# A two-layer hybrid decoder trunk: LoRA over 96 stacked rows, the norm's weights spread by all rows, and a new order of the shifts around the key norm

## The reference

```python
def rwkv7_time_mix(p, mu, w0, w2, a0, a2, k_k, k_a, r_k, lnx_w, lnx_b):
    p = p + (token_shift(p) - p) * mu
    r, k, v, wl, al = jnp.split(p, [G, 2 * G, 3 * G, 3 * G + L], axis=-1)
    decay = jnp.exp(-RWKV_DECAY_SCALE * jax.nn.sigmoid(w0 + jnp.tanh(wl) @ w2))
    a = jax.nn.sigmoid(a0 + al @ a2)
    kk = (k * k_k).reshape(B, T, H, N).astype(jnp.float32)
    kk = kk / jnp.maximum(jnp.sqrt(jnp.sum(kk * kk, axis=-1, keepdims=True)), 1e-12)
    k = k * (1.0 + (a - 1.0) * k_a)
    ...
```

## Time and profile before

| | us |
|---|---|
| median of 3 runs | 575.93 |
| lowest and highest | 575.54, 576.25 |
| the profiled execution's own time | 576.12 |
| its span in the profile | 574.3 |
| TensorE busy (share of the span) | 565.8 (99%) |
| VectorE, ScalarE, POOL busy | 379.9, 277.8, 249.5 |

### The profile page before, as it was taken

The page is one execution under the profiler, slowest core; times in us unless marked ns, Lnnn a source line. Parts: engine busy times, 40 slices in busy tenths (PEclk is TensorE's granted clock), DMA queues, the critical chain, the costliest instruction groups (busy, mean ns, idle before and its releaser), DMA issues. The chain is left out here.

```text
span 574.3 us, 12717 instructions
## 1 busy us (share of the span) xinstructions
PE 565.8 (99%) x5230; PEld 461.7 (80%) x5230; DVE 379.9 (66%) x644; ACT 277.8 (48%) x555; POOL 249.5 (43%) x197
## 2 busy tenths in 40 slices
PE   8999999999999999999999999999999999999995
PEld 6978888888877777888898788888888777788884
DVE  4989986482488557774444897947436865778173
ACT  6486241343574474534657643324357335735253
POOL 4937552044941322536335455402386313145340
PEclk9999999999999999999999999999999999999999
DMA  9546634056432122354544433332743321224513
GB/s 281 160 125 204 218 99 111 9 130 149 107 81 75 39 75 72 100 180 130 162 123 134 111 78 107 89 69 59 163 128 80 79 71 39 73 75 147 181 43 143
DMA packets 103374, 64.58 MB, mean 112 GB/s; under 512 B 29152, under 2 KB 94228, under 8 KB 103317
## 3 DMA queue, kind: packets, MB, share of 16 engines
q1 hardware_dynamic: 103316, 63.77, 39.9%
HBM read 55.61 MB, written 8.14 MB: 111 GB/s over the span
## 5 line engine op out<-in xcount | busy, mean ns | idle before, releaser
L706 POOL TENSOR_TENSOR w_lo<-w_raw,w_hi 128x512 fp32r<-128x512 f32 x156 | 216.7, 1408 | 282.2 <-ACT w_hi L1307 280.7
L770 PE MATMUL bank<-act_hi,w_hi 128*128 128x512 f32 x432 | 173.2, 401 | 0.0
L773 PE MATMUL bank<-act_lo,w_hi 128*128 128x512 f32 x432 | 168.5, 390 | 0.0
L772 PE MATMUL bank<-act_hi,w_lo 128*128 128x512 f32 x416 | 162.3, 390 | 0.0
L1307 ACT ACTIVATE w_hi<-w_raw 128x512 fp32r<-128x512 f32 x140 | 80.2, 621 | 78.3 <-PE bank L869 28.2
L770 PEld LDWEIGHTS bank<-act_hi,w_hi 128*128 128x128 f32 x432 | 81.1, 188 | 24.8 <-issue 8.4
L773 PEld LDWEIGHTS bank<-act_lo,w_hi 128*128 128x128 f32 x432 | 81.1, 188 | 17.4
L772 PEld LDWEIGHTS bank<-act_hi,w_lo 128*128 128x128 f32 x416 | 78.2, 188 | 14.9
L1233 PE MATMUL bank<-w_hi,act_hi 128*128 128x512 f32 x128 | 50.0, 391 | 0.0
L1235 PE MATMUL bank<-w_hi,act_lo 128*128 128x512 f32 x128 | 49.8, 389 | 0.0
L1234 PE MATMUL bank<-w_lo,act_hi 128*128 128x512 f32 x128 | 49.8, 389 | 0.0
(11 more groups left out here) (223 smaller groups left out, 946.2 us busy)
## 6 DMA issues: line engine op xcount, KB each, us to landing
w_raw<-in_w_in_dram SPq DMA_DIRECT2D x62, 512.0 KB, 4.0
w_raw<-in_w_out_dram SPq DMA_DIRECT2D x16, 512.0 KB, 3.8
pages<-in_x_dram SPq DMA_DIRECT2D x4, 512.0 KB, 6.2
x_or_y<-in_x_dram SPq DMA_DIRECT2D x4, 512.0 KB, 3.9
x_scratch<-x_or_y SPq DMA_DIRECT2D x4, 512.0 KB, 3.1
x_or_y<-x_scratch SPq DMA_DIRECT2D x4, 512.0 KB, 3.7
out_dram<-pages SPq DMA_DIRECT2D x8, 256.0 KB, 2.2
bias_scratch<-pages SPq DMA_DIRECT2D x1, 1280.0 KB, 7.5
```

Source lines behind the costliest of these rows:

```text
L706: ins = pool.tensor_tensor(low, raw, w_hi[:, i % HI, k, 0:n].bitcast(F32), ALU.subtract)
L770: mm(b[:, :], hi, act_hi[:, k, :], start=n == 0, stop=False)
L772: mm(b[:, :], lo, act_hi[:, k, :], start=False, stop=False)
L773: ins = mm(b[:, :], hi, act_lo[:, k, :], start=False, stop=n == KT - 1)
```

## The change

It changes five things. LoRA: the weights of both products are rounded and stacked in 96 rows as high, low and high, the inputs as high, high and low, so that one matmul in the one-pass format does what full precision did; the parts are made by a copy on ScalarE and a subtraction on VectorE (weights, first layer only) and by four copies on ScalarE and two subtractions on VectorE (inputs). The start: the norm's row lies on top of a page of zeros, so the ones span 128 rows; that load and the bias table's are issued by ScalarE, after the page has been cleared by VectorE and POOL; six idle products instead of four. The bias: the last two parts of its rows are made before the first norm, the second behind r0. The key norm: `kk_unit` is cut in two, with r1's shift between the parts. The order: LoRA comes behind v0, the decay scan behind v1, and the split parts and the product of the bonus move behind the next copies.

```diff
@@ layer_steps
-          ("kk_norm",), ("kk_unit", 0), ("lora_tanh",), ("shift", "r1"), ("kk_unit", 1), ("lora",), ("shift", "v0"), ("decay_scan",), ("shift", "v1"),
+          ("kk_norm",), ("kk_unit", 0), ("lora_tanh",), ("lora_low",), ("shift", "r1"), ("kk_scale", 0), ("shift", "v0"), ("lora",), ("kk_unit", 1), ("kk_scale", 1), ("shift", "v1"), ("decay_scan",),
           ("decay_exp",), ("factors", 0), ("gate", "rwkv", 0), ("factors", 1), ("gate", "rwkv", 1), ("factors", 2)]
 
-    s += [("copy", "rq0"), ("copy", "rq1"), ("bonus",), ("rotate", "rq0"),
-          ("copy", "rk0"), ("rotate", "rq1"), ("scores", 0), ("scores", 1), ...
+    s += [("copy", "rq0"), ("rkv_parts",), ("copy", "rq1"), ("rotate", "rq0"),
+          ("copy", "rk0"), ("rotate", "rq1"), ("bonus",), ("scores", 0), ("scores", 1), ...
@@ buffers
-        lora_w = sb("lora_w", [4 * LORA, DEPTH, P])
+        lora_w = sb("lora_w", [3 * LORA, 2, DEPTH, G], F32R)
-        norm_row = page(10)[0:1]
+        norm_rows = page(10)
+        lora_raw = page(2)[0:3 * LORA].rearrange("p (z l c) -> p z l c", z=2, l=DEPTH)
@@ SP
-            load(norm_row, norm_w[0:1, :], "norm_loaded")
-            load(bias_table, rel_bias.partition_broadcast(P), "bias_in")
-            for p in range(2):
-                for r, w in ((2 * p, rwkv_w2), (2 * p + 1, rwkv_a2)):
-                    load(lora_w[r * LORA:(r + 1) * LORA], w[:, :, p * P:(p + 1) * P].rearrange("l k c -> k l c"), "const_b")
+            for r in range(3):
+                for z, w in enumerate((rwkv_w2, rwkv_a2)):
+                    load(lora_raw[r * LORA:(r + 1) * LORA, z], w.rearrange("l k c -> k l c"), "lora_loaded")
@@ POOL
+            pool.memset(norm_rows[:, T:2 * T], 0.0).then_inc(s("norm_clear"), 1)
@@ TensorE
-            idle(4)
+            idle(6)
-                end(mm(b[:, :], one[0:1, :].to_broadcast([1, P]), norm_row[:, a * T:(a + 1) * T], start=True, stop=True), f"nw{a}", -1)
+                end(mm(b[:, :], one.to_broadcast([P, P]), norm_rows[:, a * T:(a + 1) * T], start=True, stop=True), f"nw{a}", -1)
...
-                    pe.wait_ge(*at("lora_in", layer))
-                    for p in range(2):
-                        for z, r0 in (("zw", 2 * p * LORA), ("za", (2 * p + 1) * LORA)):
-                            b = begin(f"{z}{p}", layer)
-                            end(mm(b[:, :], lora_w[r0:r0 + LORA, layer, :], WA[r0:r0 + LORA, :], start=True, stop=True, tile_position=(r0, 0)), f"{z}{p}", layer)
+                    for p in range(2):
+                        for z, name in enumerate(("zw", "za")):
+                            pe.wait_ge(*at("lora_in", layer, 2 - z))
+                            b = begin(f"{name}{p}", layer)
+                            end(mm(b[:, :], lora_w[:, z, layer, p * P:(p + 1) * P], stat_hi[0:3 * LORA, z, :], start=True, stop=True), f"{name}{p}", layer)
@@ ScalarE
+            act.wait_ge(s("norm_clear"), 2)
+            act.dma_start(norm_rows[0:1], norm_w[0:1, :]).then_inc(s("norm_loaded"), 16)
+            act.dma_start(bias_table, rel_bias.partition_broadcast(P)).then_inc(s("bias_in"), 16)
...
+                    if layer == 0:
+                        act.wait_ge(s("lora_loaded"), 16 * 6)
+                        go(lora_w.rearrange("p z l c -> p (z l c)"), lora_raw.rearrange("p z l c -> p (z l c)"), ACT.Copy).then_inc(s("lora_weight"), 1)
...
-                    go(WA[2 * LORA:4 * LORA], WA[0:2 * LORA], ACT.Copy).then_inc(s("lora_copied"), 1)
-                    act.wait_ge(*at("lora_copied", layer))
-                    for r0 in (0, 2 * LORA):
-                        go(WA[r0:r0 + LORA], WA[r0:r0 + LORA], ACT.Tanh).then_inc(s("lora_in"), 1)
+                    go(WA[0:LORA], WA[0:LORA], ACT.Tanh).then_inc(s("lora_bent"), 1)
+                    for z in (1, 0):
+                        if z == 0:
+                            act.wait_ge(*at("lora_bent", layer))
+                        for r in range(2):
+                            go(stat_hi[r * LORA:(r + 1) * LORA, z, :], WA[z * LORA:(z + 1) * LORA], ACT.Copy).then_inc(s("lora_high"), 1)
@@ VectorE
+            dve.memset(norm_rows[:, 0:T], 0.0).then_inc(s("norm_clear"), 1)
             dve.memset(bias_rows[:, :, T:DIST], MASKED)
...
+            dve.wait_ge(s("bias_in"), 16)
+            bias_runs(2)
+            bias_runs(3)
             for two in (0, 2):
...
                         if layer == 0:
-                            bias_runs(3)
+                            dve.wait_ge(s("lora_weight"), 1)
+                            low = slice(LORA, 2 * LORA)
+                            tt(lora_w[low], lora_raw[low], lora_w[low].bitcast(F32), ALU.subtract).then_inc(s("lora_weight"), 1)
...
-                    if layer == 0 and job in ("k0", "k1"):
-                        bias_runs(int(job[1]))
+                    if layer == 0 and job in ("k0", "r0"):
+                        bias_runs(0 if job == "k0" else 1)
...
                     link(dve.reciprocal(KN[:, p, :], KN[:, p, :]))
+
+                def kk_scale(p):
                     stt(KN[:, p, :], K[:, p, :], par[:, layer, KKP + p:KKP + p + 1], KN[:, p, :], ALU.mult, ALU.mult).then_inc(s("kk_unit"), 1)
+
+                def lora_low():
+                    for z in (1, 0):
+                        dve.wait_ge(*at("lora_high", layer, 4 - 2 * z))
+                        r = slice(z * LORA, (z + 1) * LORA)
+                        tt(stat_hi[2 * LORA:3 * LORA, z, :], WA[r], stat_hi[r, z, :].bitcast(F32), ALU.subtract).then_inc(s("lora_in"), 1)
```

More of the change, by code:

```diff
@@ L145, in layer_steps @@
     s += [("shift", "k0"), ("shift", "k1"), ("kk_input",), ("shift", "wa"), ("shift", "r0"), ("kk_square",),
-          ("kk_norm",), ("kk_unit", 0), ("lora_tanh",), ("shift", "r1"), ("kk_unit", 1), ("lora",), ("shift", "v0"), ("decay_scan",), ("shift", "v1"),
+          ("kk_norm",), ("kk_unit", 0), ("lora_tanh",), ("lora_low",), ("shift", "r1"), ("kk_scale", 0), ("shift", "v0"), ("lora",), ("kk_unit", 1), ("kk_scale", 1), ("shift", "v1"), ("decay_scan",),
           ("decay_exp",), ("factors", 0), ("gate", "rwkv", 0), ("factors", 1), ("gate", "rwkv", 1), ("factors", 2)]
-    s += [("copy", "rq0"), ("copy", "rq1"), ("bonus",), ("rotate", "rq0"),
-          ("copy", "rk0"), ("rotate", "rq1"), ("scores", 0), ("scores", 1), ("copy", "rk1"), ("rotate", "rk0"), ("to_rows", "v"), ("scores", 2),
+    s += [("copy", "rq0"), ("rkv_parts",), ("copy", "rq1"), ("rotate", "rq0"),
+          ("copy", "rk0"), ("rotate", "rq1"), ("bonus",), ("scores", 0), ("scores", 1), ("copy", "rk1"), ("rotate", "rk0"), ("to_rows", "v"), ("scores", 2),
           ("scores", 3), ("wide", 0, 0), ("wide", 0, 1), ("rotate", "rk1"), ("wide", 0, 2), ("wide", 0, 3),
@@ L901, in kk_square @@
                     if layer == 0:
-                        pe.wait_ge(s("const_b"), 16 * 6)
+                        pe.wait_ge(s("const_b"), 16 * 2)
                         pe.wait_ge(s("mean_r"), 1)
@@ L1327, in shift @@
                     else:
+                        if job == "v0" and layer == 0:
+                            act.wait_ge(s("lora_weight"), 2)
                         go(dst[0:n], ps(job, layer)[0:n, :], ACT.Identity, scale=der[0:n, layer, c:c + 1]).then_inc(done(job, layer), 1)
@@ L1367, in decay_exp, with rkv_parts @@
                         go(PI[:, p, :], TH[:, p, :], ACT.Exp, scale=0.5 * DECAY).then_inc(s("decay_exp"), 1)
-                def factors(part):
-                    for p in range(2) if part == 2 else ():
+                def rkv_parts():
+                    for p in range(2):
                         act.wait_ge(*full(f"kk{p}", layer))
@@ L1619, in out_end @@
                     weight_high("out7", layer)
-                run = dict(wide=wide, wide_out=wide_out, shift=shift, kk_input=kk_input, kk_norm=kk_norm, lora_tanh=lora_tanh, lora=lora, factors=factors,
+                run = dict(wide=wide, wide_out=wide_out, shift=shift, kk_input=kk_input, kk_norm=kk_norm, lora_tanh=lora_tanh, lora=lora, rkv_parts=rkv_parts,
                            decay_exp=decay_exp, gate=gate, copy=copy, to_rows=to_rows,
@@ L1656, in low, with bias_runs @@
                         .then_inc(done(f"h{t}{a}", layer - 1), 1)
+            dve.memset(norm_rows[:, 0:T], 0.0).then_inc(s("norm_clear"), 1)
             dve.memset(bias_rows[:, :, T:DIST], MASKED)
+            runs = bucket_runs()
+            def bias_runs(part):
+                for bucket, start, stop in runs[part * len(runs) // 4:(part + 1) * len(runs) // 4]:
+                    ins = dve.tensor_copy(bias_rows[:, :, start:stop], bias_table[:, bucket, :].unsqueeze(2).to_broadcast([P, HEADS, stop - start]))
+                if part == 1:
+                    ins.then_inc(s("bias_rows"), 1)
+            dve.wait_ge(s("bias_in"), 16)
+            bias_runs(2)
+            bias_runs(3)
             for two in (0, 2):
@@ L1667, in _ @@
                     low(t, 0, (a,))
[L1669 to L1678, removed]
```

(9 more changed lines are left out.)

7 lines of the change are left out of this document (4 added, 3 removed).

## The result

The changed kernel takes 585.57 us (median of 6 runs, 584.93 to 586.12) against 575.9 before (575.54 to 576.25): ratio 1.0163, 95% interval 1.0152 to 1.0174. That is 9.7 us slower; 579.1 was forecast. The profiled execution took 585.41 us around a span of 583.6, 9.3 more than before.

The account below looks back on a forecast made before the run. TensorE, busy 565.8 of 574.3 us, was taken as the bound. Start and key norm -0.16, LoRA -0.62 and two stalls +4.0 gave +3.2 us: 579.3 us in a profile, 579.1 as median, range 577.2 to 581 us.

Parts of the forecast that it names:

- the largest term in its mechanism: VectorE late at rq1 because the decay scan stands behind v1's shift: two stalls, +4.0 us in all.
- the signs: Expected if right: waits of 1 to 3 us at each rq1, scan 1.4 us behind ScalarE's v1 start, matmuls 0.23 us apart.
- signs of being wrong: rq1 on cadence despite a late scan, a bias table wait reaching TensorE, or key norm's means over 0.5 us later.
- The start: First transposes and norm: 0.8 us gained at best, 0.5 carried, of which 0.16 us gain at the key norm.
- hides the issue of two loads: At the start: ScalarE, idle until x lands at 5.03 us, hides issuing two loads; between nothing and 0.5 us if late.
- The faster transposes: At the start: an earlier higher clock makes four transposes take 0.52 instead of 0.91 us, 0.13 us apart.
- The stalls: TensorE waits at rq1 for VectorE's second gate: 1.9 us in the first layer, 2.1 in the second.
- my turns with POOL: Replay of VectorE's instructions alternating with POOL's splits; second layer's stall becomes 2.95 - 0.8 = 2.1 us, first taken as 1.9.
- The first splits meet the scan exactly as v0's did: Replay step at the decay scan: POOL's first splits, with v1's tile as zero, meet the scan as before.
- worse: Rival: no savings by turns, bias table late, a wait at rq0; 6 to 8 us of stalls, 581 to 583 us; chance 0.15.
- LoRA: Four one-pass matmuls over 96 rows, 0.91 us, replace eight passes: 0.25 + 0.37 = 0.62 us gained over both layers.
- lie under the projections of r1 and v0: Before LoRA's new place: the added subtractions and ScalarE's four copies are covered by those projections.

Follow-up runs that it names:

- Kernels 5: The changed kernel with both gates of the rwkv part ahead of the second part of the decay factors: 580.42 us, ratio 1.0069 to before.
- 7: Kernel 5 with the bias table's load and all its copies as before, the norm's row still spread: 579.68 us, 1.0057.
- 8: Kernel 5 with both the norm's row and the bias table as before: 578.58 us, 1.0040.
- kernels 2: The changed kernel with the order of before in the first part of a layer (key norm's second half, LoRA, v0, decay scan, v1): 587.41 us, 1.0196.
- 9: The changed kernel with the decay scan ahead of v1's shift: 581.36 us, 1.0092.
- kernel 1: The kernel before with one edit, the decay scan behind v1's shift: 583.99 us, ratio 1.0140.
- third kernel: Kernel 2 with the norm's row as before: first on SyncE's queue, one row of the array, 4 idle products: 586.47 us, 1.018.
- kernel 4: The third kernel with the 16 bias copies moved behind the roundings of all four tiles: 588.55 us, 1.0217.
- 6: Kernel 5 with the norm's row as before and the bias table's load behind ScalarE's first square root: 579.89 us, 1.0063.

## Why the prediction was wrong

The sign was right, and the largest term in its mechanism; the sum missed by 6 us, in these steps. Of the signs, the two waits at rq1 came, and the scan started 1.41 us behind ScalarE's start on v1's tile (1.4 forecast). But two of the signs of being wrong came too: the wait for the bias table reached TensorE, and the key norm's means came 2.69 us later.

*The start* (forecast -0.5, of which 0.16 were left at the key norm): the step that failed most. I wrote that ScalarE's idle time "hides the issue of two loads". It hides the issue, not the landing. From issue to use the row takes 4.1 us, the bias table 5.9. The table's copies stand ahead of VectorE's first reciprocal, and the row's products ahead of VectorE's first product with x, which the transposes need. With those 2.57 us and 0.12 at the key norm (where ScalarE's copy of LoRA's weights took 1.04 us as counted), the key norm is 2.69 late instead of 0.16 early: 2.85 us. Kernels 5, 7 and 8 show both waits. The faster transposes didn't come in the profiled execution, where the clock rose at 15.2 us; in kernels 2, 5 and 9, whose start is the same, it rose at 10.1, 10.0 and 4.2.

*The stalls* (forecast 1.9 and 2.1): 2.36 and 2.37, and the mechanism is shown by kernel 1. From the scan's start to the gate's end it is 17.05 us in each layer, where my turns with POOL gave 16.65 and 16.9. The scans start 14.83 us ahead of rq1's due time (14.74 by my numbers), so 2.22 us, and 0.15 from the gate's end to the product, which I had left out. The replay held in the second layer and was 0.4 us short in the first. There I had written that "The first splits meet the scan exactly as v0's did". They met more of it in this layer: its first instruction took 1.81 us instead of 1.12 and its two sums 3.31 instead of 2.34, 1.7 us more from start to start, of which the two scalings behind them gave back 1.3. The line of the sums before:

```profile
53.90 2.34 DVE L1739 TENSOR_TENSOR_SCAN pages<-constants,pages 128x512 f32<-128x512 f32 x2
```

With 0.22 at rq0, which was in the rival "worse" only, the term was 0.95 us too small.

*What a stall does to the clock* was put at nothing, without a reason. It was 1.6 us in the profiled execution. The mean clocks of the six runs are 0.992 to 0.996, against 0.998; a fall of 3.41 us at half speed is 1.7 of 583.6 us, 0.003, so they are those of one to two falls. Yet the runs at 0.993 take hardly longer than the profiled one at 0.996. What they gained elsewhere, perhaps by an earlier rise at the start, no trace shows, so the sum below holds for the profiled execution alone.

*LoRA* (forecast -0.37 and -0.25): -0.22 in the second layer, as forecast. In the first +0.16. I wrote that the added subtractions "lie under the projections of r1 and v0". They end 0.44 us too late, one of them 1.67 us long beside a split.

These misses add up to 2.85 + 0.95 + 1.6 + 0.56 = 6.0 us. 579.3 in a profile becomes 585.3; 585.41 was measured.

The rival "worse" had 581 to 583 us, with the bias table and a wait at rq0 in it, at a chance of 0.15. Both came, but its 6 to 8 us of stalls did not (4.95 us), and it too was short of the clock.

## What to carry to other kernels

Where a load is moved, count to its landing and ask who stands behind it in program order, not whether its issue is hidden. Two waits that lie side by side hide each other: undoing one gives only a part (1.9 of 2.6 us for the table here), so undo both too. Price a stall of TensorE with the slower products behind it, and before copies are moved off one engine's path, look at who waits for their end on a load queue.

## What the runs showed of the hardware

- **The clock behind a wait.** In the middle of the kernel it fell at TensorE's waits of 5.7 us (three kernels), 3.8, 2.9 and 2.0 us, and at two of the four waits of 2.2 us (changed kernel and kernel 1); in these traces it did not at waits of 1.5 us or less. A fall lasts 3.41 or 6.83 us, with 512-column products 0.43 us apart instead of 0.23.
- **The clock at the start.** With the norm's row spread over 128 rows, the record has the rise at 15.2 us in the changed kernel, but at 4.2, 8.6, 10.0 and 10.1 us in kernels 9, 7, 5 and 2. With one row it lies between 9.9 and 16.1 us in ten traces. In the third kernel TensorE waited 3.0 us from 6.8 us on and then did nothing but transposes until 13.4, and the clock rose at 12.6: the last steps between them are 0.11 instead of 0.21 us. The Trainium skill (TensorE: Matmul & The Clock Gate, Part 4), cited ahead, says that transposes do not count as activity; this trace does not agree.
- **Small copies are slowed beside POOL as well.** 16 one-column copies took 1.24 us with POOL idle, 0.08 us each, and 4.60 us beside its splits (changed kernel and kernel 4).
- **Who is issued first.** The 64 KB bias table, broadcast to 128 rows, goes with x's first tile at 7.2 to 7.7 us instead of about 5 when it was issued ahead of x's load, at 0.7 to 1.1 us (kernels 3, 4 and 6). Issued at 2.06 to 2.08, behind x's, it left x at 4.3 to 4.7 us and landed itself at 8.0 to 9.1 (changed kernel and kernels 2, 5 and 9).
